# New job orders for the four mixers, the fold on VectorE, and scores that alternate row halves

## What is computed

```python
# first block, per layer l
x = layer_norm(ALPHA * x + 0.5 * swiglu_ffn(x, ffn1_w_gu[l], ffn1_w_down[l]), ln1_g[l], ln1_b[l])
x = layer_norm(ALPHA * x + hybrid_mixer(x, w_in[l], w_out[l], attn_sinks[l], ...), ln2_g[l], ln2_b[l])
x = layer_norm(ALPHA * x + 0.5 * swiglu_ffn(x, ffn2_w_gu[l], ffn2_w_down[l]), ln3_g[l], ln3_b[l])
# hybrid_mixer: h = x @ w_in -> qa, ka, va, qr, kr, vr, gr
y_attn = sliding_window_sink_attention(rope(qa), rope(ka), va, sinks)        # 8 query heads, 2 key heads
y_ret = multiscale_retention(rotate(qr), rotate(kr), vr, gr)                 # 8 heads, group norm, silu gate
return concat(y_attn, y_ret) @ w_out
# second block, per layer l
mod = silu(c) @ w_ada[l] + b_ada[l]; shift, scale, gate = split(mod, 3)
h = x * (1 + scale) + shift; p = split(h @ w_in[l], 13 parts)
o_a = mla_attention(...)        # 6 heads, queries and keys of 64 + 32 from RMS-normed latents
o_b = dilated_attention(...)    # 6 heads, three dilated patterns in one table of log counts
o_c = sparse_attention(...)     # 4 heads, the 64 keys of 256 that an indexer scores highest
y = concat(o_a, o_b, o_c) * silu(p_gate)
x = layer_norm(ALPHA * x + (1 + gate) * (y @ w_out[l]), ln_g[l], ln_b[l])
```

## Time and profile before

| what | value |
| --- | --- |
| median of 3 runs | 1503.93 us (1500.06 to 1505.28) |
| profiled execution | 1510.47 us, of which the span is 1508.7 us |
| mean granted TensorE clock | 0.959 |
| busy: TensorE, VectorE, ScalarE, GpSimd | 1397.3, 986.0, 647.1, 182.5 us |
| mixers, stages 1, 4, 6, 7 | 146, 143, 214, 212 us |

### The profile page before, as it was taken

How to read it: one execution, slowest core, us unless ns; L and a number is a source line. 1 busy time by engine, 2 the same in 40 slices (tenths; PEclk the granted TensorE clock), 3 DMA queues, 4 the chain that set the end, 5 groups by cost and what they waited for, 6 DMA issues and landing times.

```text
span 1508.7 us, 18402 instructions
## 1 busy us (share of the span) xinstructions
PE 1397.3 (93%) x7084; PEld 1181.1 (78%) x7084; DVE 986.0 (65%) x1502; ACT 647.1 (43%) x1015; POOL 182.5 (12%) x209
## 2 busy tenths in 40 slices
PE   8999997889999999999978899899999987999886
PEld 7888876767888878888767678788798976789775
DVE  5667677366777667676764667676864865756655
ACT  5443435324443434444353244334454544455441
POOL 1011005100011010110052000410010300100000
PEclk9999999899999999999989999999999998999898
DMA  8967554118667567766442177665484413655220
GB/s 252 313 218 229 197 196 134 62 56 257 224 210 237 188 218 242 230 210 217 163 144 84 56 249 233 219 226 196 149 281 124 141 52 91 222 162 159 87 84 28
DMA packets 174855, 265.41 MB, mean 176 GB/s; under 512 B 16496, under 2 KB 131312, under 8 KB 174256
## 3 DMA queue, kind: packets, MB, share of 16 engines
q1 hardware_dynamic: 163056, 223.63, 45.6%
q0 software_dynamic: 11712, 40.60, 8.2%
HBM read 263.13 MB, written 1.07 MB: 175 GB/s over the span
## 4 chain that ended last, share of the span: by engine, by line
PE 70%; DVE 16%; ACT 6%; DMA 5%; issue 2%; POOL 1%; SPq 0%; DVEq 0%; POOLq 0%
PE ps L730 21%; PE ps L731 20%; PE ps L732 20%; DVE w_lo L1185 8%; PE ps L799 3%; ACT w_hi L1026 3%; DMA w_raw<-in_w_in 2%; PE ps L971 2%; ACT att L1131 2%; DMA w_raw<-in_ffn_w_gu 2%; PE ps L942 2%; DVE att L1349 1%; DVE small L1359 1%; DVE col_lo L1197 1%; DVE small L1215 1%
## 5 line engine op out<-in xcount | busy, mean ns | idle before, releaser
L1185 DVE TENSOR_TENSOR w_lo<-w_raw,w_hi 128x1024 fp32r<-128x1024 f32 (+3 forms) x424 | 509.8, 1246 | 315.8 <-ACT w_hi L1026 314.5
L1026 ACT ACTIVATE w_hi<-w_raw 128x1024 fp32r<-128x1024 f32 (+3 forms) x424 | 419.1, 1040 | 281.4 <-DMA w_raw<-in_ffn_w_gu 167.5
L730 PE MATMUL ps<-w_hi,col_hi 128*128 128x512 f32 (+2 forms) x1216 | 490.7, 403 | 21.1 <-DVE col_lo L1197 12.9
L731 PE MATMUL ps<-w_lo,col_hi 128*128 128x512 f32 (+2 forms) x1216 | 475.1, 391 | 0.0
L732 PE MATMUL ps<-w_hi,col_lo 128*128 128x512 f32 (+2 forms) x1216 | 474.8, 390 | 0.0
L730 PEld LDWEIGHTS ps<-w_hi,col_hi 128*128 128x128 f32 x1216 | 235.0, 193 | 74.9 <-DVE w_lo L1185 16.8
L732 PEld LDWEIGHTS ps<-w_hi,col_lo 128*128 128x128 f32 x1216 | 234.2, 193 | 47.8
L731 PEld LDWEIGHTS ps<-w_lo,col_hi 128*128 128x128 f32 x1216 | 235.4, 194 | 42.5
L730 PE MATMUL ps<-w_hi,lat_hi 128*128 128x512 f32 (+2 forms) x416 | 158.0, 380 | 0.0
L732 PE MATMUL ps<-w_hi,lat_lo 128*128 128x512 f32 (+2 forms) x416 | 156.5, 376 | 0.0
L731 PE MATMUL ps<-w_lo,lat_hi 128*128 128x512 f32 (+2 forms) x416 | 156.5, 376 | 0.0
(11 more groups left out here) (145 smaller groups left out, 1328.0 us busy)
## 6 DMA issues: line engine op xcount, KB each, us to landing
w_raw<-in_ffn_w_gu SPq DMA_DIRECT2D x172, 512.0 KB, 5.2
w_raw<-in_w_in SPq DMA_DIRECT2D x54, 1024.0 KB, 5.3
w_raw<-in_ffn_w_down SPq DMA_DIRECT2D x44, 1024.0 KB, 5.3
mod<-in_w_ada POOLq DMA_DIRECT2D x32, 768.0 KB, 7.6
w_raw<-in_w_out SPq DMA_DIRECT2D x16, 1024.0 KB, 4.9
norm_g<-in_ln_g POOLq DMA_DIRECT2D x8, 512.0 KB, 4.6
...
```

The costliest lines, as they stand in the source:

```text
L730: pe.matmul(dst, a_hi, b_hi, start=start, stop=False)
L731: pe.matmul(dst, a_hi, b_lo, start=False, stop=False)
L1026: act.activation(half_of(w_hi[j], n, h), half_of(raw[j], n, h), ACT.Copy).then_inc(hi_ready, 1)
L1185: tt(half_of(w_lo[j], n, h), half_of(raw[j], n, h), half_of(w_hi[j], n, h).bitcast(F32), ALU.subtract)\
```

## The change

- `mix1_jobs` and `mix2_jobs` return one written order each, `MIX1_ORDER` and `MIX2_ORDER`, for both layers. The order of the units stays; most jobs of a mixer change places. A word with + belongs to the next stage.
- The splits are jobs of their own, `hi` for ScalarE and `lo` for VectorE, one for each half of a unit. Those that an order doesn't place, in the feed-forward stages above all, `with_splits` puts where the old rule had them.
- `fold` is done by VectorE in three instructions instead of by GpSimd in four. In stage 5 it stands two rounds after `modload`, in stage 6 near the stage's end, after `turn:C:1`.
- In `idx`, `score` and `ret` the loops over pairs and halves change places, and both semaphore increments come with the last pair.
- `neg_max` and `row_sum` exist for each group A, B, C. The first `out` waits for whatever last held its banks. The rotation of the retention stays on GpSimd.

```diff
@@ -161,7 +161,9 @@
             jobs += down(lag, 0) + down(lag, 1)
             lag += 1
         if r == 4 and s == FIRST2 - 1:
-            jobs += [("modload", FIRST2), ("fold", FIRST2)]
+            jobs += [("modload", FIRST2)]
+        if r == 6 and s == FIRST2 - 1:
+            jobs += [("fold", FIRST2)]
     if s == FIRST2 - 1:
         jobs += [("gains", FIRST2)]
...
+MIX1_ORDER = """
+hi:QR/0:0 lo:QR/0:0 hi:QR/0:1 row:KV:0:0 hi:QR/1:0 row:QA:0:0 lo:QR/0:1 row:QA:0:1 xt:1 params rope:0 row:QR:0:0
+row:KV:1:0 hi:QR/1:1 hi:KR/0:0 lo:QR/1:0 row:QA:1:0 row:QA:1:1 lo:QR/1:1 hi:KR/0:1 tr:0 row:QR:0:1 lo:KR/0:0
+hi:KR/1:0 lo:KR/0:1 hi:KR/1:1 rope:1 hi:VR/0:0 row:QR:1:0 lo:KR/1:0 score:W:0 row:KR:0:0 row:QR:1:1 hi:VR/0:1
+lo:KR/1:1 hi:VR/1:0 row:KR:0:1 tr:1 hi:VR/1:1 row:KR:1:0 lo:VR/0:0 lo:VR/0:1 score:W:1 turn:W:0 hi:GR/0:0
+lo:VR/1:0 lo:VR/1:1 row:KR:1:1 score:W:2 lo:GR/0:0 row:VR:0:0 rot:Q:0 mix:W:0 turn:W:1 hi:GR/0:1 rot:Q:1
+hi:GR/1:0 hi:GR/1:1 hi:out/0:0 rot:K:0 rot:K:1 row:VR:0:1 hi:out/0:1 row:VR:1:0 trret:Q:0 trret:Q:1 lo:GR/0:1
+mix:W:1 turn:W:2 hi:out/1:0 row:VR:1:1 trret:K:0 mix:W:2 hi:out/1:1 lo:GR/1:0 lo:GR/1:1 lo:out/0:0 attn:0 attn:1
+trret:K:1 ret:0 hi:out/2:0 row:GR:0:0 lo:out/0:1 ret:1 retmix:0 gn:0 ret:2 lo:out/1:0 row:GR:0:1 gnx:0 hi:out/2:1
+row:GR:1:0 ycols:0:0 hi:out/3:0 retmix:1 hi:out/3:1 gn:1 ycols:0:1 lo:out/1:1 lo:out/2:0 lo:out/2:1 row:GR:1:1
+out:0:0 gnx:1 lo:out/3:0 lo:out/3:1 +hi:gu/0/0:0 +hi:gu/0/0:1 ycols:1:0 out:1:0 out:2:0 ycols:1:1 out:0:1
++lo:gu/0/0:0 +hi:gu/0/1:0 +lo:gu/0/0:1 out:3:0 out:1:1 norm:0 +xt:0 +lo:gu/0/1:0 +lo:gu/0/1:1 +lo:gu/1/0:0
++lo:gu/1/0:1 +hi:gu/0/1:1 out:2:1 out:3:1 +hi:gu/1/0:0 +hi:gu/1/0:1 norm:1
+"""
+
+MIX2_ORDER = """
+table2 row:L0:0:0 hi:L1/1:0 lo:L1/1:0 hi:L1/1:1 row:L0:0:1 row:L1:0:0 lo:L1/1:1 xt:1 row:L1:0:1 hi:QB/0:0
+hi:QB/0:1 sq:0 row:L0:1:0 hi:QB/1:0 hi:QB/1:1 xlate:0 xlate:1 lo:QB/0:0 lo:QB/0:1 latent:0 row:L0:1:1 params
+lo:QB/1:0 row:L1:1:0 row:L1:1:1 hi:QB/2:0 hi:QB/2:1 trlat:0:0 T:QB:0 hi:VBX/0:0 hi:VBX/0:1 hi:VBX/1:0 lo:QB/1:1
+trlat:0:1 lo:QB/2:0 lo:QB/2:1 hi:VBX/1:1 lo:VBX/0:0 lo:VBX/0:1 sq:1 lo:VBX/1:0 latent:1 lo:VBX/1:1 hi:QI/0:0
+T:QB:1 T:QB:2 row:VBX:0:0 lo:QI/0:0 lo:QI/0:1 hi:QI/0:1 hi:QI/1:0 trlat:1:0 score:B:0 trlat:1:1 lo:QI/1:0
+row:VBX:0:1 hi:QI/1:1 hi:KI/0:0 hi:KI/0:1 row:VBX:1:0 row:VBX:1:1 lo:QI/1:1 turn:B:0 score:B:1 hi:UQ/0:0
+hi:UQ/0:1 idxw:0 gateload lo:KI/0:0 lo:KI/0:1 T:QI:0 score:B:2 mix:B:0 turn:B:1 lo:UQ/0:0 lo:UQ/0:1 lo:UQ/1:0
+T:QI:1 T:KI:0 hi:UQ/1:0 mix:B:1 hi:UQ/1:1 idxw:1 lo:UQ/1:1 idx:0 lo:UKV/0:0 lo:UKV/0:1 hi:UKV/0:0 +modload
+lo:VC/0:0 hi:UKV/0:1 hi:VC/0:0 hi:VC/0:1 row:UQ0:0:0 lo:VC/0:1 row:UQ0:1:0 turn:B:2 lo:QC/0:0 hi:QC/0:0
+row:UQ1:0:0 lo:QC/0:1 hi:QC/0:1 idx:1 ropeA:0 hi:QC/1:0 row:UQ1:1:0 ropeA:1 row:UV:0:0 idx:2 row:UV:1:0 topk:0:0
+row:UK:0:0 row:UK:1:0 ropeK:0 ropeK:1 topk:0:1 lo:QC/1:0 lo:QC/1:1 topk:0:2 hi:QC/1:1 hi:G0/0:0 trA:0 row:VC:0:0
+trA:1 trA:2 topk:0:3 hi:G0/0:1 hi:G0/1:0 row:VC:1:0 trA:3 trA:4 trA:5 lo:G0/0:0 hi:G0/1:1 mix:B:2 score:A:0
+lo:G0/0:1 hi:G1/0:0 hi:G1/0:1 hi:G1/1:0 hi:G1/1:1 T:QC:0 score:A:1 lo:G0/1:0 topk:1:0 T:QC:1 topk:1:1 turn:A:0
+topk:1:2 score:A:2 lo:G0/1:1 lo:G1/0:0 row:G0:0:0 turn:A:1 mix:A:0 topk:1:3 row:G0:0:1 lo:G1/0:1 hi:out/0:0
+turn:A:2 lo:G1/1:0 hi:out/0:1 score:C:0 mix:A:1 row:G1:0:0 row:G1:0:1 lo:G1/1:1 lo:out/0:0 lo:out/0:1 row:G0:1:0
+swish:0 score:C:1 gate:0:0 turn:C:0 mix:A:2 row:G0:1:1 row:G1:1:0 turn:C:1 +fold mix:C:0 gate:0:2 lo:out/1:0
+hi:out/1:0 hi:out/1:1 row:G1:1:1 gate:0:1 ycols:0:0 lo:out/1:1 mix:C:1 swish:1 gate:1:1 ycols:0:1 ycols:0:2
+gate:1:0 out:0:0 lo:out/2:0 gate:1:2 hi:out/2:0 ycols:1:0 lo:out/2:1 lo:out/3:0 hi:out/2:1 ycols:1:1 out:1:0
+out:2:0 hi:out/3:0 lo:out/3:1 hi:out/3:1 +hi:L0/0:0 ycols:1:2 out:3:0 norm:0 +lo:L0/0:0 out:0:1 out:1:1 +xt:0
++hi:L0/0:1 +hi:L0/1:0 +lo:L0/0:1 +lo:L0/1:0 out:2:1 +hi:L0/1:1 out:3:1 +hi:L1/0:0 +lo:L0/1:1 +lo:L1/0:0
++lo:L1/0:1 +hi:L1/0:1 norm:1
+"""
+
+
+def listed(order, s):
+
+    def part(w):
+        return tuple(part(v) for v in w.split("/")) if "/" in w else int(w) if w.isdigit() else w
+
+    jobs = []
+    for w in order.split():
+        to = s + (w[0] == "+")
+        if to < len(KIND):
+            kind, *rest = w.lstrip("+").split(":")
+            jobs.append((kind, to, *(part(v) for v in rest)))
+    return jobs
+
+
 def mix1_jobs(s):
-    r = lambda name, i: row(s, name, i)
...
+    return listed(MIX1_ORDER, s)
 def mix2_jobs(s):
+    return listed(MIX2_ORDER, s) + ([("gains", s + 1)] if s < LAST else [])
...
+def with_splits(jobs):
+
+    units, first, last, streamed = uses(jobs)
+    placed, places, at = set(jobs), [[] for _ in jobs], 0
+    for n, u in enumerate(units):
+        if n < FIRST_UNITS:
+            continue
+        if n < SLOTS:
+            due = n * UNIT + 1
+        else:
+            assert last[units[n - SLOTS]] < first[u]
+            given = streamed[last[units[n - SLOTS]] + 1]
+            due = max(given + SPLIT_BEHIND - UNIT, min(given + SPLIT_BEHIND, streamed[first[u]] - 2 * UNIT))
+        while at < first[u] and streamed[at] < due:
+            at += 1
+        assert at <= first[u]
+        places[at] += [(kind, *u, h) for h in range(2) for kind in ("hi", "lo") if (kind, *u, h) not in placed]
+    return [q for p, job in zip(places, jobs) for q in p + [job]]
+
+
+JOBS = with_splits(JOBS)
+UNITS, FIRST_USE, LAST_USE, _ = uses(JOBS)
+NUMBER = {u: n for n, u in enumerate(UNITS)}
+for kind_ in ("hi", "lo"):
+    assert [q[1:] for q in JOBS if q[0] == kind_] == [(*u, h) for u in UNITS[FIRST_UNITS:] for h in range(2)], "split in order"
...
+            if job[2:] == (0, 0):
+                for h in range(2):
+                    BANK_BEFORE[s, "out", 0, h] = held[4 + h]
...
-        if kind in ("latent", "sq", "swish", "rope", "rot", "idx", "idxw", "ropeA", "ropeK", "fold", "modsum", "modrow"):
+        if kind in ("latent", "sq", "swish", "rope", "rot", "idx", "idxw", "ropeA", "ropeK", "modsum", "modrow"):
             COUNT.add(kind, job)
+        if kind == "fold":
+            COUNT.add(kind, job, 2)
...
-        neg_max = few(TT * 8).rearrange("p (t h) -> p t h", t=TT)
-        row_sum = few(TT * 8).rearrange("p (t h) -> p t h", t=TT)
+        neg_max = {g: few(TT * 8).rearrange("p (t h) -> p t h", t=TT) for g in "ABC"}
+        row_sum = {g: few(TT * 8).rearrange("p (t h) -> p t h", t=TT) for g in "ABC"}
+        neg_max["W"], row_sum["W"] = neg_max["A"], row_sum["A"]
...
                     toks = slice(i * P, (i + 1) * P)
-                    for half in range(2):
-                        rows = slice(64 * half, 64 * half + 64)
-                        for q, pair in enumerate(pairs):
+                    for q, pair in enumerate(pairs):
+                        for half in range(2):
+                            rows = slice(64 * half, 64 * half + 64)
...
                                 a, b = qa_t[0:A_HD, 2 * pair + half, toks], ka_t[0:A_HD, 2 * pair + half, 0:keys]
                             last = pe.matmul(ps[:, half, q * keys:(q + 1) * keys], a, b, start=True, stop=True)
-                        last.then_inc(scores, 1)
+                            if pair == pairs[-1]:
+                                last.then_inc(scores, 1)
...
-                            pe.wait_ge(copied, at["copied", (s, "GR" if KIND[s] == "mix1" else "G1", h)])
+                            bank_ready((s, "out", 0, h))
...
                     first_split((0, 1) if j == 0 else range(2, FIRST_UNITS * FIRST_KS))
-                for n in SPLITS[j]:
-                    split(n)
                 kind, s = job[:2]
-                if kind == "xt":
+                if kind == "hi":
+                    split(NUMBER[job[1:3]], job[3])
+                elif kind == "xt":
...
-            def split(n):
+            def split(n, h):
                 j = SLOT[n]
-                for h in range(2):
-                    dve.wait_ge(hi_ready, 2 * (n - FIRST_UNITS) + h + 1)
-                    tt(half_of(w_lo[j], n, h), half_of(raw[j], n, h), half_of(w_hi[j], n, h).bitcast(F32), ALU.subtract)\
-                        .then_inc(lo_ready, 1)
+                dve.wait_ge(hi_ready, 2 * (n - FIRST_UNITS) + h + 1)
+                tt(half_of(w_lo[j], n, h), half_of(raw[j], n, h), half_of(w_hi[j], n, h).bitcast(F32), ALU.subtract)\
+                    .then_inc(lo_ready, 1)
 
...
+                elif kind == "fold":
+                    dve.wait_ge(mod_in, at["mod_in", s])
+                    dve.wait_ge(params_in, at["params_in", s - 1])
+                    both = shift_scale(s)
+                    shift2, scale2 = both[:, 0:D], both[:, D:2 * D]
+                    halves = lambda v: v.rearrange("p (a b) -> p a b", a=2)
+                    spare = prob_t if s == FIRST2 else lat_spare
+                    if s > FIRST2:
+                        dve.wait_ge(copied, at["copied", (s - 1, "UV", 1)])
```

(18 more changed lines are left out.)

152 lines of the change are left out of this document (44 added, 108 removed).

## The result

The changed kernel takes 1372.07 us (median of 4 runs, 1371.22 to 1373.00), the kernel before 1504.61 (4 runs, 1500.06 to 1507.43): ratio 0.9124, 95% interval 0.9106 to 0.9142, 132.5 us faster. The forecast was 1404 us, in a range of 1376 to 1470: right in sign, 32 us short in size, and 4 us outside the range at its fast end. The profiled execution took 1373.0 us.

A forecast was written before the change was run, and what follows sets the result against it. TensorE's streaming bounds the feed-forward stages; the mixers lose 139 us to idle time and lowered clock, caused by order. Gains of 87 + 8 + 5 = 100 us: 1510.5 - 100 - 6.5 = 1404 us, range 1376 to 1470.

The forecast's parts named there:

- goes by the orders: Four mixers: the new orders and places remove 87 us of idle time and lost clock, bounds 70 to 119.
- fold, stage 5: Second mixers' feeding stage: fold off GpSimd sends the next `w_ada` chunk earlier; net gain 8 us, bounds 4 and 8.4.
- alternation: Score, idx and ret in the mixers: alternating row halves overlaps their records; gain 5 us, bounds 0 and 6.4.
- nearly everything goes: Rival for the mixers: only 5 to 7 us left per mixer, 1370 to 1385 us; chance 0.12.
- The pool: Four mixers: TensorE idle time plus work lost to the clock, without the last norm's tail, 139 us a reordering can draw from.
- The named waits: Mixers: TensorE waits such as 8.3 us before a score, y's 6.2 and 7.7, and copies, to go or shrink.
- The signs of being right: First mixers 114 to 122 us, second 180 to 190, clock 0.96 or more, fold stage 193, W:0 and `ret` about 1.1.
- One sign of being wrong: Mixers: the prediction is wrong if `w_hi` or `w_lo` becomes the releaser of TensorE's waits; no size given.
- What stays per mixer ... 7. To that I add 6 us for what I have not foreseen: Each mixer keeps 7 us of waits and clock plus 6 us for unforeseen late landings or copies: 13, 52 in all.
- the slower rival: Mixers: `w_hi` entries ahead of copies wait for landings, at most 8.7 us each; 1517 or 1543 us; chance 0.03.
- The common cause: Mixers: splits come as blocks of a whole unit, placed by streamed columns, ahead of small work on the chain.
- The 6.5 us taken off: End of the sum: the profiled execution, 1510.5 us, lay 6.5 us over the runs' median, 1503.9, so this is subtracted.

The follow-up runs named there:

- the first two of the three edits above: Changed kernel with QB/2 and G1/1 `w_lo` halves earlier, VBX/1:0 `w_hi` later in second mixers; 1364.73 us with `xt:0` a job later, 1368.16 with `out:3:0` before `out:0:1` instead.
- The shifted halves: Changed kernel with its 316 placed halves moved past one more row, T or out job: ahead (276 move) 1452.69 us, behind (298 move) 1426.20 us.

## Where the prediction was right, and the step that failed

| term | forecast | measured |
| --- | --- | --- |
| stays in the four mixers | 52 | 12 |
| goes by the orders | 87 | 124.4 |
| fold, stage 5 | 8 | 8.0 |
| alternation | 5 | 6.1 |
| other stages | 0 | -1.0 |
| from the profiled execution to the median | 6.5 | 0.9 |

The 12 are 1.9 + 1.9 + 4.1 of idle time, and 12.8 less the tail of 8.7, with no clock lost. The 124.4 are 130.5 less the alternation, 0.55 us in each of ten jobs and 0.3 in two; the experiments give 122 for the same. The forecast is 1510.5 - 100 - 6.5; measured, 1510.5 - 137.5 - 0.9. What came is the rival "nearly everything goes" (1370 to 1385, chance 0.12), with still less left per mixer than its 5 to 7 us.

- **The pool was right.** 139 us less the 12 that stay is 127, and 124 went; the 3 us between lie within the rounding of the four clocks to two digits (0.005 of 715 us is 3.6). What was read from the four rows as idle time and lost clock was what a reordering could draw from.
- **The named waits went as counted,** the 8.3 us before line 942, y, the copies of the turned probabilities and of `lat_rows`, each to nothing or 0.3 us, two of them further than counted. The signs of being right hold: clock 0.99 and 1.00, stage 5 at 192.3 us, no wait of VectorE for `in_w_ada`, W:0 and `ret` at 1.16 us. One sign of being wrong came too: in the second mixers `w_lo` releases nearly all of TensorE's waits that are left. They are short, 3.5 and 3.1 us a stage, and with the first two of the three edits above, which move `w_lo` halves ahead, 0.5 us of them is left in each. The second mixers came at 181 and 182 us, within the 180 to 190 given, the first at 111, under the 114 to 122.
- **The step that failed is "What stays per mixer ... 7. To that I add 6 us for what I have not foreseen"**, 13 us where 1.9 to 4.1 stayed. It has three parts. Of the 6 us not foreseen, 24 in all, nothing came in the first mixers and 3 to 3.5 us, the waits for `w_lo`, in the second. The 2 to 3 us of clock beside waits of 1 to 2 us were not there: waits of up to 1.5 us stand in the trace after, and the clock is 1.00 around them. And the waits named as staying were shorter: `tr:1` and `trA` left 0 and 0.3 us, not 1 to 2, the head of a first mixer 0.4, not 1.4; only the wait of a first mixer for `xt` was 1.4, as counted.
- **Why the reserve was wrong is shown only in part.** Its ground was that separately placed halves are fragile. The shifted halves show that they are: one job earlier or later costs 81 or 54 us, and the mechanism of the slower rival (`w_hi` waiting for its landing ahead of other work) costs 8.9 us at one place. But the orders as written miss such places nearly everywhere, at `tr:1` by 0.1 us. That no wait stands there rests on 0.1 us which the count did not show, and is luck. I traced a handful of chains and found them fitting, and still charged the others as if they were placed by chance.
- **The common cause was half of it.** "Splits come as blocks" holds for 61 us with the new job order and 26 with the old. The larger part is the job order: 61 us alone, and without it the waits for `lat_rows`, y and the copies are back. The prediction counted, chain by chain, the jobs that the new order gives TensorE meanwhile, but named only the splits as the cause.
- **In stage 6 only the fold's cost on VectorE was priced, 0 to 1 us;** what it does there beside VectorE's work while GpSimd has it was put at nothing. With the new orders, leaving it on GpSimd costs 5.8 us. How much of stage 6's gain in the change is the fold's stays open: in the old order stage 6 went from 214.1 to 208.4 us with the fold moved, but from 210.3 to 211.9 with the alternation there already, each in one execution.
- **The 6.5 us taken off hid part of the miss.** The profiled execution of before lay that far above its median, and the runs of that kernel spread over 12 us (1498.5 to 1510.8), those of the changed one over 1.8 (four runs). The spread goes with the clock: over 37 executions of the kernel before, beside the versions above, the time rises as the mean granted clock falls (correlation -0.91), from 1498.5 us at 0.967 to 1510.8 at 0.957. So it is part of what the orders remove, and subtracting it counts it twice; the changed kernel's profiled execution lies only 0.9 us above its median. This went 5.6 us the other way: without it the forecast is 1410.5 us, farther off, so the terms missed by 37 us, and that the forecast missed by only 32 is the luck of a second error. That the waits are what moves the clock from run to run is argued from the pairs of waits at the end, not shown.
